# Softmax in steps of two heads: scores side by side on array rows, values as stationary side by side on its columns

## The reference, cut to what matters

```python
# window: 8 heads of 64; latents see a window of the latents (bias) and all of the context
s_win = einsum(q, k_win) * scale + bias;  s_ctx = einsum(q, k_ctx) * scale
p = softmax(concat([s_win, s_ctx]));      o = p_win @ v_win + p_ctx @ v_ctx
# context: 8 heads of 64, dense, 256 keys
# mla: 8 heads; scores from 128 + 64 dimensions, values of 128
s = (einsum(qn, kn) + einsum(qr, kr)) * scale;  o = softmax(s) @ v
# banded: 8 heads of 64, three groups of keys under three masks (window, dilation), one softmax over all
```

## Time and profile before

| | us |
|---|---|
| median of three runs | 2780.46 (2780.4 to 2781.45) |
| the profiled execution | 2779.02 |
| its span | 2777.2 |
| TensorE matmul, busy | 2601.9 (94%), 15266 records |
| TensorE weight load, busy | 2203.3 (79%) |
| VectorE, busy | 1595.9 (57%) |
| ScalarE, busy | 465.3 (17%) |
| chain that ended last, share of TensorE | 90% (L1746 to L1748 70%, L1927 3%, L1953 2%) |

### The profile page before, as it was taken

One profiled execution on the slowest core, in us unless ns is written; L12 is line 12 of the kernel. 1 busy time (PEld: TensorE's weight loads), 2 busy tenths in 40 slices (PEclk: granted clock), 3 DMA queues, 4 the chain that ended last, 5 costly groups with the idle time before them and its releaser, 6 DMA issues.

```text
span 2777.2 us, 38234 instructions
## 1 busy us (share of the span) xinstructions
PE 2601.9 (94%) x15266; PEld 2203.3 (79%) x15266; DVE 1595.9 (57%) x2429; ACT 465.3 (17%) x926; POOL 5.0 (0%) x12
## 2 busy tenths in 40 slices
PE   5999999999999999999997999999996896889998
PEld 2777777777777777888886479989885895889998
DVE  3544445334544444654446358886765667759976
ACT  2000001132100000211002331111452211111101
POOL 0000000000000000000000000000000000000000
PEclk9999999999999999999998899999997998889999
DMA  5544444301444444222222115545321221325553
GB/s 217 190 175 166 176 175 156 101 1 45 152 163 173 179 174 161 91 94 102 91 98 62 53 69 196 180 160 180 126 88 38 77 92 46 122 94 189 186 190 110
DMA packets 88986, 356.75 MB, mean 128 GB/s; under 512 B 9825, under 2 KB 11105, under 8 KB 79393
## 3 DMA queue, kind: packets, MB, share of 16 engines
q1 hardware_dynamic: 86976, 349.32, 36.0%
q0 software_dynamic: 848, 4.67, 0.5%
q10 hardware_dynamic: 1040, 1.05, 0.1%
HBM read 353.95 MB, written 1.05 MB: 128 GB/s over the span
## 4 chain that ended last, share of the span: by engine, by line
PE 90%; DVE 6%; ACT 1%; DMA 1%; issue 1%; SPq 0%; DVEq 0%; ACTq 0%
PE lin L1746 24%; PE lin L1747 23%; PE lin L1748 23%; PE pair L1927 3%; PE pair L1849 3%; PE lin L1953 2%; PE lin L1795 1%; DMA raw_all<-w_ada 1%; PE lin L1796 1%; PE lin L1799 1%; PE lin L1754 1%; PE pair L2244 1%; PE pair L2233 1%; PE lin L1756 1%; PE lin L1755 1%
## 5 line engine op out<-in xcount | busy, mean ns | idle before, releaser
L1746 PE MATMUL lin<-h_all,whi 128*128 128x256 f32 (+1 forms) x2608 | 873.5, 335 | 10.3 <-DVE wlo L1293 6.6
L1747 PE MATMUL lin<-h_all,whi 128*128 128x256 f32 (+1 forms) x2608 | 863.0, 331 | 0.0
L1748 PE MATMUL lin<-h_all,wlo 128*128 128x256 f32 (+1 forms) x2608 | 862.6, 331 | 0.0
L1293 DVE TENSOR_TENSOR wlo<-raw_all,whi 128x1024 fp32r<-128x1024 f32 (+1 forms) x529 | 635.9, 1202 | 20.3 <-ACT whi L1156 2.6
L1292 DVE CAST whi<-raw_all 128x1024 fp32r<-128x1024 f32 (+2 forms) x508 | 344.2, 678 | 409.0 <-PE lin L1748 355.4
L1746 PEld LDWEIGHTS lin<-h_all,whi 128*128 128x128 f32 x2608 | 500.0, 192 | 94.8 <-issue 41.9
L1748 PEld LDWEIGHTS lin<-h_all,wlo 128*128 128x128 f32 x2608 | 499.5, 192 | 45.1
L1747 PEld LDWEIGHTS lin<-h_all,whi 128*128 128x128 f32 x2608 | 500.1, 192 | 42.7
L1746 PE MATMUL lin<-a_all,whi 128*128 128x256 f32 (+1 forms) x1148 | 388.8, 339 | 34.8 <-DVE a_all L1340 33.3
L1747 PE MATMUL lin<-a_all,whi 128*128 128x256 f32 (+1 forms) x1148 | 385.0, 335 | 0.0
L1748 PE MATMUL lin<-a_all,wlo 128*128 128x256 f32 (+1 forms) x1148 | 384.6, 335 | 0.0
(11 more groups left out here) (285 smaller groups left out, 2175.8 us busy)
## 6 DMA issues: line engine op xcount, KB each, us to landing
raw_all<-w_up SPq DMA_DIRECT2D x176, 512.0 KB, 3.5
raw_all<-w_ada SPq DMA_DIRECT2D x72, 1024.0 KB, 4.8
raw_all<-w_down SPq DMA_DIRECT2D x64, 512.0 KB, 3.5
raw_all<-w_exp_up SPq DMA_DIRECT2D x64, 512.0 KB, 3.5
raw_all<-w_exp_down SPq DMA_DIRECT2D x32, 512.0 KB, 3.5
raw_all<-w_down SPq DMA_DIRECT2D x32, 384.0 KB, 2.9
raw_all<-w_b_qk SPq DMA_DIRECT2D x24, 512.0 KB, 3.5
raw_all<-w_b_conv SPq DMA_DIRECT2D x24, 512.0 KB, 3.4
```

The lines of the kernel that those rows point to most:

```text
L1293: dve.tensor_tensor(wlo[s][:, 0:n], r[:, 0:n], whi[s][:, 0:n].bitcast(F32), ALU.subtract)\
L1746: pe.matmul(out_, a, hi[n], start=start and n == 0, stop=False)
L1747: pe.matmul(out_, a, lo[n], start=False, stop=False)
L1748: ins = pe.matmul(out_, b, hi[n], start=False, stop=stop and n == len(cols) - 1)
```

## The change

`softmaxes` goes by steps u of two items, 2u and 2u + 1, an even and an odd head, on all three engines.

- ScalarE's order inside a step is, for each half, the convolution's early part, the exponential of item 2u + half, the middle part, the copy of turned item 2u + half - 2, and the late part.
- Scores of both items are issued alternately, product by product, into two banks. They wait for the exponential of item 2u - 2 (banded: the maximum of item 2u - 1).
- Value products wait for both items. The values are stationary, the turned exponentials move, and the result lies with the value's dimensions on partitions: for heads of 64 the even head on partitions 0 to 63 and the odd one on 64 to 127 of the same columns, issued alternately.
- `turn_group` goes. Instead `spread_sums` multiplies the four columns of inverted sums, broadcast, with the identity, so that each lies along the row of its head. ScalarE copies the group's result to SBUF (`copy_values`), VectorE multiplies it there with the spread rows, ScalarE makes the high part and VectorE the low part from SBUF.
- Reciprocals are a step of their own (`invert_sums`) on VectorE, before the group's scaling.
- Beside banded, the convolution runs two steps ahead; each step has two of its units, one behind the scores and one behind the value products, and the second item's transposes come last. On VectorE the second item's maximum comes behind the first unit's work.
- The root and the reciprocal norms of the delta tiles come one slot earlier (18, 19), spreads and scalings start in slot 20 instead of 21, all eight are in the loop, and the rows go round three banks, two of them score banks.

```diff
-            return (pair[0][:, 1], pair[1][:, 0])[n % 2] if kind == "qk" else lin[:, 3]
+            return (pair[0][:, 1], pair[1][:, 0])[n % 2] if kind == "qk" else (lin[:, 3], pair[0][:, 0], pair[0][:, 1])[n % 3]
...
+        def value_out(bank, dv, c):
+            half = slice(64 * (c % 2), 64 * (c % 2) + 64) if dv == 64 else slice(0, P)
+            at = c // 2 if dv == 64 else c
+            return bank[half, at * P:(at + 1) * P]
```

On ScalarE:

```diff
+                def copy_values(g):
+                    kind, (dv, _, _) = groups[g]
+                    act.wait_ge(S("o_full"), (n0 + 4 * g) // 2 + 2)
+                    if g >= 2:
+                        act.wait_ge(S("ot_done"), g0 + g - 1)
+                    act.activation(wide(out_tiles(kind, dv, g)), o_bank(kind, g)[:, 0:2 * P if dv == 64 else 4 * P], ACT.Copy)\
+                        .then_inc(S("o_copied"), 1)
+                for u in range(-lead, N // 2 + 3):
+                    if u >= 4 and u % 2 == 0:
+                        copy_values((u - 4) // 2)
+                    for half in range(2):
...
+                    if u >= 4 and u % 2 == 0:
+                        high_part(groups, (u - 4) // 2, g0)
```

On VectorE:

```diff
+                for u in range(-lead, N // 2 + 3):
+                    aside = beside if u + lead < STEPS_BESIDE else None
+                    if u >= 3 and u % 2:
+                        if (u - 3) // 2 < N // 4:
+                            invert_sums((u - 3) // 2, n0, g0)
+                    for half in range(2):
+                        if 0 <= 2 * u + half < N:
+                            maximum(2 * u + half)
+                        if half and u >= 4 and u % 2 == 0:
+                            scale_group(groups, (u - 4) // 2, n0, g0)
+                        if aside:
+                            aside(2 * (u + lead) + half, "middle")
+                            aside(2 * (u + lead) + half, "late")
+                    if u >= 5 and u % 2:
+                        low_part(groups, (u - 5) // 2, g0)
             def scale_group(groups, g, n0, g0):
-                dve.tensor_tensor(view(W(BUFFERS[kind][2], 2, 4 * dv)[:, g % 2], (4, dv)), view(o_bank(kind, g)[:, 0:4 * dv], (4, dv)),
-                                  inverse_sums(g0 + g).unsqueeze(2).broadcast_to([P, 4, dv]), ALU.mult)\
+                dve.wait_ge(S("rows_spread"), g0 + g + 1)
+                dve.wait_ge(S("o_copied"), g0 + g + 1)
+                dve.tensor_tensor(out_, out_, row_bank[:, 0:cols], ALU.mult)\
                     .then_inc(S("o_scaled"), 1)
```

On TensorE:

```diff
+                def scores(t):
+                    kind = items[t][0]
+                    if kind == "banded":
+                        if t < 8:
+                            pe.wait_ge(S("qk_scaled"), 12)
+                        if t:
+                            pe.wait_ge(S("max_ready"), n0 + t)
+                    elif t:
+                        pe.wait_ge(S("exp_ready"), n0 + t - 1)
+                    both = (items[t][1][0], items[t + 1][1][0])
+                    for q in range(len(both[0])):
+                        for m, ops in enumerate(both):
+                            a, b, lhs, rhs = ops[q]
...
+                            ins = pe.matmul(score_bank(kind, t + m)[:, a:b], lhs, rhs, start=first, stop=last)
+                def value_products(m):
...
+                    pe.wait_ge(S("turned_read"), n0 + m + 2)
+                    if m % 4 == 0 and g >= depth:
+                        pe.wait_ge(S("o_copied"), g0 + g + 1 - depth)
+                    side_by_side = [(c, kt) for kt in range(K) for c in range(2)]
+                    for c, kt in side_by_side if dv == 64 else sorted(side_by_side):
+                        turned = W(BUFFERS[kind][1], 3, 512)[:, (m + c) % 3]
+                        ins = pe.matmul(value_out(o_bank(kind, g), dv, (m + c) % 4), values[c][kt], turned[:, kt * P:(kt + 1) * P],
+                                        start=kt == 0, stop=kt == K - 1)
+                def spread_sums(g):
...
+                    for c in range(4):
+                        ins = pe.matmul(value_out(row_bank, dv, c), inverse_sums(g0 + g)[:, c:c + 1].to_broadcast([P, dv]), ident,
+                                        start=True, stop=True)
+                for u in range(-lead, N // 2 + 2):
+                    aside = beside if u + lead < STEPS_BESIDE else None
+                    if 0 <= u < N // 2:
+                        scores(2 * u)
+                    if aside:
+                        aside(2 * (u + lead))
+                    if 1 <= u <= N // 2:
+                        turn(2 * u - 2)
+                        if not beside:
+                            turn(2 * u - 1)
+                    if u >= 2:
+                        value_products(2 * u - 4)
+                        if u % 2:
+                            spread_sums((u - 3) // 2)
+                    if aside:
+                        aside(2 * (u + lead) + 1)
+                    if beside and 1 <= u <= N // 2:
+                        turn(2 * u - 1)
```

More of the change, by code:

```diff
@@ L1108, in softmaxes @@
                 lead = LEAD if beside else 0
[L1109 to L1134, removed]
@@ new lines, in maximum @@
+                def maximum(t):
+                    kind, (_, cols, mask, _) = items[t]
+                    dve.wait_ge(S("scores_full"), n0 + t + 1)
+                    if mask is None:
+                        dve.tensor_reduce(neg_max(n0 + t), score_bank(kind, t)[:, 0:cols], AX.X, ALU.max, negate=True)\
+                            .then_inc(S("max_ready"), 1)
+                    else:
+                        if t >= 3:
+                            dve.wait_ge(S("exp_ready"), n0 + t - 2)
+                        dve.tensor_tensor_reduce(W(B_SC, 3, 512)[:, t % 3, 0:cols], score_bank(kind, t)[:, 0:cols], mask,
+                                                 -NA_SCALE, -NEG, ALU.add, ALU.min, neg_max(n0 + t))\
+                            .then_inc(S("max_ready"), 1)
@@ L1925, in softmaxes @@
                             last = all(o[1] <= a or o[0] >= b for o in ops[q + 1:])
                             first = all(o[1] <= a or o[0] >= b for o in ops[:q])
-                            ins = pe.matmul(score_bank(kind, t)[:, a:b], lhs, rhs, start=first, stop=last)
-                        ins.then_inc(S("scores_full"), 1)
-                    if beside:
-                        beside(t + lead)
-                    if 0 <= t - 2 < N:
-                        m = t - 2
-                        kind, (_, cols, _, _) = items[m]
-                        depth = 1 if kind == "banded" else 2
-                        pe.wait_ge(S("exp_ready"), n0 + m + 1)
-                        if m >= depth:
-                            pe.wait_ge(S("turned_read"), n0 + m + 1 - depth)
-                        p = W(BUFFERS[kind][0], 3, 512)[:, m % 3]
-                        for kt in range(cols // P):
-                            ins = pe.transpose(turn_bank(kind, m)[:, kt * P:(kt + 1) * P], p[:, kt * P:(kt + 1) * P], ident)
-                        ins.then_inc(S("turned_full"), 1)
@@ L1942, in softmaxes @@
-                    if 0 <= t - 3 < N:
-                        m = t - 3
-                        kind, (_, _, _, values) = items[m]
-                        depth = 1 if kind == "banded" else 2
-                        g, c = divmod(m, 4)
-                        dv = values[0].shape[1]
-                        pe.wait_ge(S("turned_read"), n0 + m + 1)
-                        if c == 0 and g >= depth:
-                            pe.wait_ge(S("o_scaled"), g0 + g + 1 - depth)
-                        turned = W(BUFFERS[kind][1], 3, 512)[:, m % 3]
-                        for kt, v in enumerate(values):
-                            ins = pe.matmul(o_bank(kind, g)[:, c * dv:(c + 1) * dv], turned[:, kt * P:(kt + 1) * P], v,
-                                            start=kt == 0, stop=kt == len(values) - 1)
-                        ins.then_inc(S("o_full"), 1)
```

147 lines of the change are left out of this document (75 added, 72 removed).

## The result

The changed kernel takes 2712.70 us (median of 4 runs, 2711.60 to 2713.65) against 2780.87 us of the kernel before on the same chip: ratio 0.9755, 95% interval 0.9738 to 0.9772. The forecast was 2730 with a range of 2716 to 2756.

A forecast was written before the change was run, and what follows sets the result against it. TensorE, 94% busy, was taken as the bound; savings of 16 (windows and context), 5.5 (mla), 20.5 (banded) and 9 (tail) sum to 51 us, taking 2780.5 to 2729.5, so 2730; range 2716 to 2756.

The forecast's parts named there:

- Scores side by side: Softmax scores of two heads overlap: window 3.18 to 2.05 us, context 1.26 to 0.66, mla 4.02 to 2.9, banded 2.14 to 1.1.
- row halves don't overlap: Rival on the scores: window gives back 7 us, mla 5, context 1, banded 8; kernel 2751; chance 0.12.
- Values in column halves: Value products of two heads of 64 overlap in column halves: 0.95 us plus 0.15 for changeovers, against 1.86.
- The rival: Column halves don't overlap in value products: window and banded give back 14 us, context 3; kernel 2747; chance 0.06.
- Windows and context: First softmax call: window steps 4.4 us against 6.1, context steps 2.3 against 2.94; 16 us saved.
- Mla: Mla softmax: steps 6.1 us against 7.0, the first 16 us at 0.50 clock unchanged; 5.5 us saved.
- Banded's 16 heads: Banded softmax, 1994.5 to 2090: steps of 9.1 us, 73.5 against 95.5 in all; 20.5 us taken as saved.
- VectorE or ScalarE bounds the banded steps: Rival: banded steps 10 us, context 2.6, half the ping-pong stays; gives back 7 + 2.5 + 5; kernel 2745; chance 0.24.
- Tail: Banded's end, 2090 to 2129.1: three banks and an earlier start remove most ping-pong, 39.1 to 30 us; 9 saved.
- The clock as a rival: Slower case: pauses in steps of two drop the softmax stretches' granted clock to 0.50; 2808 with half affected; chance 0.05.

The follow-up runs named there:

- lighter tail: The changed kernel with the last group's copy and scaling a slot earlier and ScalarE making high parts in the tail too: 2713.06 us, ratio 0.9755.

## Why the prediction was right and wrong

**Scores side by side: right.** The forecast had the second head's passes hidden wholly, by the column strips of the earlier trace rows. The window's 2.05 (its terms 0.87, 0.2 and 0.96 add up to 2.03) measured 2.03, the context's 0.66 was 0.63, mla's 2.9 was 2.87, banded's 1.1 was 1.08. The rival "row halves don't overlap" was made real and cost 20.1 us; it had been priced at 21.

**Values in column halves: right.** 0.95 to 1.1 was forecast, 0.93 to 1.02 came. The rival cost 18.0, priced at 17. By the rule that the prediction took from the Trainium skill, "TensorE: Matmul & The Clock Gate", Part 3, these loads should not overlap, since all use the same rows; the trace disagrees, 1.02 us against 1.89 with one column half, and the load records of the two halves start 6 to 7 ns apart.

**Windows and context, 19.3 instead of 16: a little short.** Windows shrank by 12.2 us (44.4 to 32.1, first score at 575.88 to the context's at 608.01), 1.3 less than forecast; context and the end of the call by 7.0 instead of 3. ScalarE was named as late next there, at 2.3 a step, with 2 more given back in the first two steps. It is busy for 22.5 of the 29.1 us from 602 on, but the steps came at 2.13, just above TensorE's own sum of 2.0.

**Mla, 11.0 instead of 5.5: the step that failed.** The forecast read the 16.1 us at 0.50 in the earlier trace rows, asked how much work is done in them, and let them stand: "in steps of two the same four are done". It took the lower clock as a property of the pause ahead of mla. It depends on the order of the products too, which the change also alters. The clock was back after 3.6 us, 12.5 us earlier. As an estimate half of that is saved work time, 6.2; the other 4.8, by subtraction, are the steps, forecast at 5.5. Without the 5.5 us by which mla beat its term the kernel would have been at 2718, inside the range. The twelve experiments show it: 3.3 to 6.8 us at 0.50 in the seven kernels in which mla's two 128-row products adjoin, 19.6 to 20.7 in the five in which they alternate with 64-row ones. The kernel before itself had 16.1 in the profile shown, but 19.6 and 19.9 in the two kernels that leave its mla as it is, so the change is worth 1 to 2 us more than that one profile says.

**Banded's 16 heads, 22.0: the sum was right** (73.5 by steps, 73.5 measured; 20.5 was taken for caution). The rival "VectorE or ScalarE bounds the banded steps", which had 0.24, was wrong: VectorE's 58.8 of 73.5 us left its slack, and TensorE waited for nothing.

**Tail, 11.3 instead of 9: the ping-pong was read rightly, its clock was left out.** The 9 us were all waits. Of the 11.3, TensorE's idle time gave 5.9 (12.6 to 6.7) and its busy time 5.4 (26.5 to 21.1), since the old ping-pong also kept 14.9 us at 1.2 GHz. So the size of the waits was too high and the clock's share was missing; that the sum came near is in part luck. By itself the new tail is worth 14.0 us; after the faster steps less (38.6 to 27.8 is 10.8), probably since the last group's copy, scaling and low part stand in it. The forecast's 30 was built on VectorE's load; VectorE is nearly full there (24.9 of 27.8), yet in the lighter tail 2.0 us less of it bring 1.0. What else stands in the tail is TensorE's 2.1 us for the reciprocals, 4.6 at the end and 5.0 at the lower clock.

**The rest, 2.5.** Between the calls nothing was forecast and -2.5 us came. In the kernels here, whose other stages are alike, the piece ahead of mla takes 905.2 to 910.1 us; the difference lies within that.

**The clock as a rival** pointed to the wrong side. It was feared to fall in steps of two, with 0.05; instead the old steps were those that hold it down. The rows for it stood in the forecast: TensorE busy for 16.10 of 16.10 us at 0.50, a stretch in which there is no pause at all.

Added up: mla 5.5 more, windows and context 3.3, the tail 2.3, banded's steps 1.5, the rest 2.5 make 15.1 of span (66.1 against 51). The medians lie 68.2 apart; the other 2.1 are the scatter of single executions.

## What to carry to other kernels

Products that use half the rows or half the columns should be paired with one that uses the other half, and issued alternately: here it took the second head's passes off the time wholly, while a full product in between undid it. A stretch in which TensorE is busy without a gap at a granted clock of 0.50 is to be priced as something that the order of its instructions can change, not as a fixed entry fee. And a change that removes pauses should be priced twice: the waits, and the clock that the pauses cost.

## What the runs showed that was not expected

The granted clock can stay at 0.50 under an unbroken chain of matmuls: 16.1 to 20.7 us in mla with 128-row and 64-row products in turn, 66.9 us in the windows of one head a step. It was back after 3.3 to 6.8 us in mla once two 128-row products adjoined, whether the 64-row pair overlapped (6.3) or not (6.8), and after 9.4 in the windows once the two heads' products lay side by side. Which property of the stream decides is open. Adjoining products on 128 rows fit mla but not the windows of one head: there biases, transposes and values, all on 128 rows, stand together in every item, and the clock stayed down for 66.9 us. A fuller array fits the windows but not mla, where it came back without overlap. Fewer changes between 64 and 128 rows fit both: twice for two heads in every stretch with an early return, four times in every one with a late return. But nothing was run to test that, and in the windows of one head the clock came back at last with the order unchanged, so no property of the order is the whole account.

A pause of TensorE of 6.3 us ahead of the windows cost the kernel before 33 us in the median, and 26 to 65 in its four executions. In the profiled one, whose span is 41.0 us longer than before, 31.8 are in the first call. In the profile before, the windows ran at 1.00 throughout; that gave no hint of how near they were to this.

Overlap needs halves that differ in the rows or in the columns, and depends on the order: 1.02 us for alternated value passes, 1.51 for the same passes one half after the other, 1.89 in one half.
